# Three edits to the order of one hybrid layer on one core: a gate product, two gate blocks, and the first expert's product in halves

## What is computed

```
proj = u @ w_in                  # -> rq, rk, rv, rg, dqkv, dz, da, db, gate_a, gate_b
o_r, s_ret = retention(q, k, v, log_gamma, s_ret)
o_r = rms_plain(o_r) * silu(rg)                 # gate product of the retention
o_d, s_dn = gated_delta(qd, kd, vd, g, beta, s_dn)
o_d = rms_plain(o_d) * dn_norm * silu(dz)       # dz: the delta rule's output gate
h = h + (sigmoid(gate_a) * (o_r @ w_ret_up) + sigmoid(gate_b) * (o_d @ w_dn_up)) @ w_out
# then a mixture of 16 experts, each:
gu = u @ w_gate_up[e]; hid = silu(gu[:, :256]) * gu[:, 256:]
moe += combine[:, e] * (hid @ w_down[e])
```

## Time and profile before

| | |
|---|---|
| three runs, us | 883.27, 883.37, 882.80; median 883.27 |
| the profiled execution, us | 883.2, its span 881.4 |
| granted TensorE clock, mean | 0.999 |
| TensorE (PE) busy | 862.2 us |
| VectorE (DVE), ScalarE (ACT), GpSimd (POOL) busy | 367.5, 223.3, 155.1 us |

### The profile page before, as it was taken

One profiled execution on the slowest core, in us unless ns is written; L12 is line 12 of the kernel. 1 busy time (PEld: TensorE's weight loads), 2 busy tenths in 40 slices (PEclk: granted clock), 3 DMA queues, 4 the chain that ended last, 5 costly groups with the idle time before them and its releaser, 6 DMA issues.

```text
span 881.4 us, 11837 instructions
## 1 busy us (share of the span) xinstructions
PE 862.2 (98%) x4657; PEld 558.1 (63%) x4657; DVE 367.5 (42%) x833; ACT 223.3 (25%) x476; POOL 155.1 (18%) x186
## 2 busy tenths in 40 slices
PE   9999999999999999999999999999999999999996
PEld 4546777888789876777777755555444444444452
DVE  3223565766556325566643542334311111104553
ACT  2211243274223210131011102120211111115554
POOL 0324320022243314201300430002000000003100
PEclk9999999999999999999999999999999999999999
DMA  9512332502020201333222244016999999785111
GB/s 359 194 75 88 132 127 106 150 1 104 1 98 3 97 2 68 135 124 134 97 106 85 97 153 184 25 49 231 394 369 366 369 362 366 282 314 170 62 46 48
DMA packets 19813, 135.98 MB, mean 154 GB/s; under 512 B 2512, under 2 KB 3024, under 8 KB 12592
## 3 DMA queue, kind: packets, MB, share of 16 engines
q1 hardware_dynamic: 12176, 103.28, 30.5%
q0 software_dynamic: 5424, 26.45, 8.4%
q10 hardware_dynamic: 2160, 5.51, 2.0%
HBM read 117.83 MB, written 21.60 MB: 158 GB/s over the span
## 4 chain that ended last, share of the span: by engine, by line
PE 44%; DVE 3%; issue 1%; ACT 1%; DMA 1%; POOLq 0%; POOL 0%; DVEq 0%; ACTq 0%
PE single L1200 12%; PE pair L1108 7%; PE pair L1189 6%; PE single L898 6%; PE pair L1302 3%; PE pair L919 2%; PE single L1177 2%; PE pair L1240 2%; PE single L919 2%; PE single L1154 1%; DMA mem<-y_slots,posu 1%; PE single L1117 1%; DVE mem L2196 0%; PE single L1213 0%; PE single L1126 0%
## 5 line engine op out<-in xcount | busy, mean ns | idle before, releaser
L718 PE MATMUL pair<-mem 128*128 128x288 f32 x640 | 158.9, 408 | 0.0
L718 PEld LDWEIGHTS pair<-mem 128*128 128x128 f32 x640 | 120.3, 190 | 35.6 <-ACT mem L1323 2.1
L1200 PE MATMUL single<-mem 128*128 128x512 f32 x256 | 112.8, 593 | 1.4 <-DVE mem L2160 1.4
L898 PE MATMUL single<-mem 128*128 128x288 f32 x448 | 110.1, 407 | 0.3
L898 PEld LDWEIGHTS single<-mem 128*128 128x128 f32 x448 | 84.7, 190 | 25.8 <-issue 1.6
L1200 PEld LDWEIGHTS single<-mem 128*128 128x128 f32 x256 | 47.3, 190 | 54.7 <-issue 53.1
L1323 ACT ACTIVATE mem<-single 128x256 f32<-128x256 f32 (+5 forms) x113 | 46.5, 421 | 132.6 <-PE single L1117 51.0
L1323 ACT ACTIVATE mem<-pair 128x512 f32<-128x512 f32 (+5 forms) x83 | 36.6, 492 | 160.0 <-PE pair L718 63.1
L2153 DVE SCALAR_TENSOR_TENSOR mem<-single,mem 128x256 f32<-128x256 f32 x16 | 7.8, 484 | 138.8 <-PE single L1200 126.3
L1108 PE MATMUL pair<-mem 128*128 128x512 f32 (+1 forms) x192 | 64.6, 527 | 0.5 <-DVE mem L2000 0.5
L1302 PE MATMUL pair<-mem 128*128 128x512 f32 (+1 forms) x192 | 63.4, 524 | 0.9 <-DVE mem L2206 0.9
(11 more groups left out here) (385 smaller groups left out, 1117.3 us busy)
## 6 DMA issues: line engine op xcount, KB each, us to landing
mem<-in_w_gu SPq DMA_DIRECT2D x16, 2048.0 KB, 9.3
mem<-in_w_down SPq DMA_DIRECT2D x16, 1024.0 KB, 11.7
y_slots<-mem SPq DMA_DIRECT2D x16, 512.0 KB, 3.5
y_slots<-in_zeros POOLq DMA_DIRECT2D x8, 512.0 KB, 8.0
mem<-in_w_ga SPq DMA_DIRECT2D x2, 2048.0 KB, 8.6
mem<-in_w_gb SPq DMA_DIRECT2D x2, 2048.0 KB, 8.1
mem<-in_w_wo SPq DMA_DIRECT2D x2, 2048.0 KB, 8.1
mem<-in_w_pg SPq DMA_DIRECT2D x2, 2048.0 KB, 11.1
```

What stands on the lines that cost most here:

```text
L718: last = nc.tensor.matmul(pb[:, hf, 0:HALF], w(k), rhs[:, k, hf * HALF:(hf + 1) * HALF], start=(k == 0), stop=(k == kk - 1))
L898: last = nc.tensor.matmul(single[plan.buf[s]][:, 0:HALF], lhs[:, k, :], rhs[:, k, :], start=(k == 0 and j in (0, 1, 3, 4)), stop=(k == 3), ...
L1200: last = nc.tensor.matmul(single[3][:, :], xT[u % 2][:, k, :], w_gu[u][:, k, :], start=(k == 0), stop=(k == KD - 1))
```

## The change

1. `rgs 0` moves on VectorE from ahead of all `gK`, `gQ` to behind `gQ 2`.
2. `dz 1` moves from behind `sU 2` to between `sU 1` and `sD 2`, and `dz 2` from behind `sU 3` to between `sU 2` and `sD 3`. `dz 3` stays.
3. The first half of the first expert's evacuation signals a semaphore of its own. The first four blocks of the first expert's product wait for that, and block 4 for the whole.

```
-    s += [("rg", 0), ("cvs", NCONV - 1), ("rgs", 0)]
+    s += [("rg", 0), ("cvs", NCONV - 1)]
     for t in range(NT):
-        s += [("gK", t), ("gQ", t)]
+        s += [("gK", t), ("gQ", t)] + ([("rgs", 0)] if t == 2 else [])
...
     s += [("sO", 0), ("sU", 0), ("dz", 0), ("sD", 1), ("sDs",), ("sO", 1), ("sU", 1),
-          ("sD", 2), ("sO4",), ("sO", 2), ("sU", 2), ("dz", 1), ("sD", 3), ("sOt",), ("sUs", 0), ("sO", 3), ("sU", 3), ("wT", 0),
-          ("dz", 2), ("sUs", 1), ("wT", 1), ("wT", 2), ("dz", 3), ("sUs", 2), ("wS", 0, 0), ("wS", 0, 1), ("sUs", 3), ("wT", 3)]
+          ("dz", 1), ("sD", 2), ("sO4",), ("sO", 2), ("sU", 2), ("dz", 2), ("sD", 3), ("sOt",), ("sUs", 0), ("sO", 3), ("sU", 3), ("wT", 0),
+          ("sUs", 1), ("wT", 1), ("wT", 2), ("dz", 3), ("sUs", 2), ("wS", 0, 0), ("wS", 0, 1), ("sUs", 3), ("wT", 3)]
...
-                pe.wait_ge(sem("xT"), e + 1)
+                if first and u == 0:
+                    pe.wait_ge(sem("xT_half"), 1)
+                else:
+                    pe.wait_ge(sem("xT"), e + 1)
                 pe.wait_ge(sem(f"wgu{u}"), xg_next[1])
...
                 for k in range(KD):
+                    if first and u == 0 and k == 4:
+                        pe.wait_ge(sem("xT"), 1)
...
+                    if first and hf == 0:
+                        last.then_inc(sem("xT_half"), 1)
                 last.then_inc(done, 1)
```

More of the change, by code:

```diff
@@ L2154, in expert_dve, with x_evac @@
                                        op0=ALU.mult, op1=ALU.mult).then_inc(sem("hid"), 1)
-            def x_evac(u, count, into, done):
+            def x_evac(u, count, into, done, first=False):
                 dve.wait_ge(sem("xT_mm"), count)
@@ L2161, in x_evac @@
                                            bc(g_ffn[:, 4 * hf:4 * hf + 4], P, 4, P), ALU.mult)
+                    if first and hf == 0:
+                        last.then_inc(sem("xT_half"), 1)
                 last.then_inc(done, 1)
-            x_evac(0, 1, xT, sem("xT"))
+            x_evac(0, 1, xT, sem("xT"), True)
             for e in range(NEXP):
```

## The result

| | before | changed |
|---|---|---|
| median of 22 runs each, us | 883.48 | 886.51 |
| lowest and highest, us | 882.29, 887.60 | 883.93, 890.24 |
| ratio, 95% interval | | 1.0033, 1.0022 to 1.0043 |
| profiled execution, us | 883.2 | 885.6 (span 883.8) |
| mean granted clock of the profiled execution | 0.999 | 0.994 |

I had forecast 883.5 us, no change that can be told, with 882.3 to 885.3 as the range. The measured median lies above that range.

What follows compares the result with a forecast made beforehand. TensorE's queue was taken as the bound from end to end. The terms -1.37 - 1.31 + 3.6 - 0.61 = +0.3 us on 883.2 gave 883.5 us, counted as no change, with a range of 882.3 to 885.3.

Steps and rivals of the forecast that it cites:

- What bounds the kernel: Whole kernel: TensorE's queue, busy 862.2 us or 98% of the span; shifts of TensorE should reach the end in full.
- Edit 1, -1.37: At `gK 2`: without the gate product ahead, VectorE's mask frees the bank in time; gain 1.37 us, bounds 1.0 and 1.6.
- Edit 2, the part that goes, -1.31: At `sD 2`: `dz 1` covers VectorE's state addition, so TensorE's wait goes; gain 1.31 us, bounds 1.2 and 1.5.
- Edit 2, the part that comes, +3.6: At `sUs 1`: without `dz 2` as cover, TensorE waits for GpSimd's `dexp`; cost 3.6 us, bounds 3.3 and 4.5.
- the chain of four links: From `sU 3` to `sUs 1`: hand-over, VectorE's state addition, GpSimd's DMA issue, `dexp`; none moves relative to `sU 3`.
- Edit 3, -0.61: At the first expert: TensorE starts after the evacuation's first half; gain 0.61 us, bounds 0.4 and 0.7.
- the sum: Whole kernel: -1.37 - 1.31 + 3.6 - 0.61 = +0.3 us, from -0.5 to +1.9 with terms at their ends.
- the clock behind the gap: Rival: the 3.6 us gap at `sUs 1` lowers TensorE's clock; 2.1 us lost, 885.6 us, chance 0.10.
- Its price, 2.1: Loss in us if 4.3 us of work in `dz 3`, behind the gap, ran at half speed.
- The rival's 885.6 us: Forecast time if the gap at `sUs 1` lowers TensorE's clock; chance 0.10.
- list of what would show it wrong: New wait under 3 or over 4 us, clock falling behind it, or another wait between 225 and 290 us.
- the trace's own end: Kernel's end: clock held through 4.8 us of idle after the last product, more than the 3.6 forecast at `sUs 1`.

Runs made afterwards that it cites:

- N = 4: Changed kernel plus four products of constants, 512 columns wide, on TensorE between `sU 3` and `sUs 1`: 884.46 us, ratio 0.9996 to the kernel before.
- the ladder above: Changed kernel with 0, 1, 2, 4 or 8 products of constants ahead of `sUs 1`: medians +3.3, +3.4, +1.6, +0.7, +3.4 us above the kernel before.
- the one without the gate blocks: Kernel before with the `rgs 0` move and the half signal, `dz 1` and `dz 2` left in place: 881.43 us, ratio 0.9971.
- the gate blocks alone: Kernel before with only the moves of `dz 1` and `dz 2`: 889.45 us, ratio 1.0063.
- N = 1: Changed kernel plus one product of constants, 512 columns wide, between `sU 3` and `sUs 1`: median 3.4 us above the kernel before.
- N = 2: Changed kernel plus two products of constants, 512 columns wide, between `sU 3` and `sUs 1`: median 1.6 us above the kernel before.
- the second profile of the changed kernel: Changed kernel run again unaltered, with no products added ahead of `sUs 1`: median 3.3 us above the kernel before.

## Why the prediction was wrong

- **What bounds the kernel: right.** The difference made between 283 and 350 us stands unchanged at 606.
- **Edit 1, -1.37: right.** The wait is gone; from the first `gK` to `rg 1` it is 8.3 us (208.34 to 216.65) for 9.95, which is 1.6, the upper bound.
- **Edit 2, the part that goes, -1.31: right.** No wait at L1032. The stage is 1.5 shorter where nothing comes in its place, again the upper bound.
- **Edit 2, the part that comes, +3.6: right.** The recorded wait is 3.47, and 3.64 from where the next product could have started (0.89 behind `sU 3`'s start, as with N = 4), by the chain of four links that was named. Moving one DMA in GpSimd's queue removes it.
- **Edit 3, -0.61: right.** The product starts 0.75 after the evacuation does (607.54 to 608.29), 1.34 before. With these measured terms the sum is -1.6 - 1.5 + 3.5 - 0.6 = -0.2, not +0.3.
- **The step that failed: the clock behind the gap, which the sum put at nothing.** It stood as a rival with a chance of 0.10, on one observation, that the clock held for 4.8 us after the kernel's last product. That row shows how the clock behaved in one place once, and I used it as if it were a length that any gap has to reach. It was near the longest of its kind: the 14 endings go from 2.2 to 5.3. In the new gap the clock fell 2.4 us after the last product, and with 1.8 us of idle it fell in most runs, by their mean clocks. In all 28 runs of the changed kernel the mean clock was 0.996 or lower, so this case was the likely one.
- **Its price, 2.1: of the right size, but low for the median.** It cost 2.8 us in the first profile and 1.7 in the second; the 22 runs put it at 2.7 (3.0 less the 0.3 of the sum), or 3.2 with the measured terms. I took the longest low stretch from the start of the kernel, 4.3 us, and halved it. In the first profile the low stretch lasted 6.8, of which TensorE worked 5.7; in the four others 3.4. The rival's 885.6 us was 0.9 short as well.
- The prediction's list of what would show it wrong had the clock's row in it, and that is where it showed.

The Trainium skill, TensorE: Matmul & The Clock Gate, section "Why this matters for your kernels", warns of exactly this, a long idle gap that brings the half clock back. The runs agree, and with the ladder above at gaps down to 1.8 us. I had set the trace's own end against the rule. Another execution's end would have shown 2.2 us, less than the gap that I forecast, so one trace's end was no fit witness.

What stays open: why waits of 1.3 and 1.4 us elsewhere in the kernel before leave the clock alone while 1.8 us at this place mostly don't, and what decides whether the clock is low for 3.4 us or 6.8. The work ahead of this gap is small products, 128 columns wide, and ahead of the wait at `sD 2` it is the same kind; I didn't run the same gap behind wide products.

The best version is the changed kernel with the prompt's state sent later, 0.9962 (0.9946 to 0.9977) of before. Against the one without the gate blocks (0.9971), its further gain of one wait (1.3 us recorded, 1.5 in the stage's length) is in the profile, but the intervals overlap.

## What to carry to other kernels

A block moved to cover one wait uncovers another: look at what stands behind it in every queue (here a DMA issue on GpSimd that nobody had waited for), and give the longest chain the cover. On a kernel whose TensorE never rests, a gap of a few us has a second price, the half clock behind it, which here was nearly as large as the gap (2.7 us beside 3.5); don't take a late fall of the clock at one execution's end as proof that a gap is harmless. If a gap must stay, products of constants in it can be cheaper than idling.

## What the runs showed of the hardware

- The granted clock can fall after the idle time is over. With 3.5 us of idle it fell within the gap once (337.9, TensorE back at 338.95). In the other four profiles it fell behind the gap: 0.6 us with the gate blocks alone, 1.3 with N = 1, 0.6 with N = 2, and 1.1 in the second profile of the changed kernel (339.8, back at 338.70):

```profile
338.70 1.13 PE L1091 MATMUL pair<-mem 32*128 32x512 f32 x4 [3.47 <-POOL mem L2399]
339.76 9.71 PE L718 MATMUL pair<-mem 128*128 128x288 f32 x32
```

- It stayed at the half level for 3.4 us in four profiles and for 6.8 in one, although TensorE was fully busy for most of it.
- No single delay fits all the falls. From the end of the last product ahead of the idle time to the fall it was 2.4 to 4.6 us in the five profiles with a gap, and 2.2 to 5.3 us at the 14 endings.
- VectorE's sums of two tensors and GpSimd's products can take longer when they overlap, and which of them does varies. In the kernel before, a sum took 3.02 us in place of 1.35 while GpSimd's state scaling beside it kept its 1.89. In the changed kernel, behind `sUs 1`, `dexp` of head 3 took 2.15 us where it took 1.04 before, the state scaling 3.00 for 1.89, and VectorE's sum 2.08 for 1.36. With N = 4, at full clock, the same three took 2.15, 3.00 and 2.08, so it isn't the clock of TensorE. No wait of TensorE came of it:

```profile
343.48 2.15 POOL L2399 TENSOR_TENSOR mem<-mem,const 64x512 f32<-64x512 f32 x1
344.76 2.08 DVE L1921 TENSOR_TENSOR mem<-mem 128x1152 f32<-128x1152 f32 x1
345.60 3.00 POOL L2402 TENSOR_TENSOR mem<-mem,glast_s 128x1024 f32<-128x1024 f32 x1
```
